# Forming a round's transposed rows by one set of products in the expert rounds of a two-block model kernel

## What is computed

```python
D_MODEL, MOE_EXPERTS, MOE_TOP_K, MOE_FF = 1024, 32, 2, 512
# every token goes to 2 of 32 experts; the tokens of an expert are its rows, padded to whole blocks
xp = jnp.zeros((nb * MOE_BLOCK, D), h.dtype).at[dest].set(h[tok_s])
def expert_block(args):
    xb, e = args
    return (jax.nn.silu(xb @ w_gate[e]) * (xb @ w_up[e])) @ w_down[e]
yp = lax.map(expert_block, ...)
return jax.ops.segment_sum(yp[dest] * w_s[:, None], tok_s, num_segments=T)
```

## Time and profile before

| | |
|---|---|
| median of 3 runs | 2140.02 us (2138.09 to 2142.48) |
| profiled execution | 2139.3 us, span on the core 2137.5 us |
| TensorE busy | 1995.6 us (93%), 9661 instructions |
| weight loads of TensorE | 1085.2 us (51%) |
| VectorE busy | 991.1 us (46%) |
| ScalarE busy | 683.1 us (32%) |
| GpSimd busy | 44.9 us (2%) |
| read from HBM | 605.06 MB, 289 GB/s over the span |
| chain that ended last | TensorE 68%, DMA 25%, VectorE 3%, ScalarE 2% |

### The profile page before, as it was taken

One profiled execution on the slowest core, in us unless ns is written; L12 is line 12 of the kernel. 1 busy time (PEld: TensorE's weight loads), 2 busy tenths in 40 slices (PEclk: granted clock), 3 DMA queues, 4 the chain that ended last, 5 costly groups with the idle time before them and its releaser, 6 DMA issues.

```text
span 2137.5 us, 29392 instructions
## 1 busy us (share of the span) xinstructions
PE 1995.6 (93%) x9661; PEld 1085.2 (51%) x9662; DVE 991.1 (46%) x2196; ACT 683.1 (32%) x1090; POOL 44.9 (2%) x80
## 2 busy tenths in 40 slices
PE   8999999999999999998999898888998999989888
PEld 4546777645577775554433343333774433334333
DVE  2375987303488544444444333344324443333335
ACT  1261000103400002142555444444202554444444
POOL 2000000000000000000000000001000000000000
PEclk9999999999999999999999999999999999999999
DMA  9505996533189543314999999999545999999996
GB/s 308 205 1 219 368 349 241 198 118 140 46 349 365 192 166 129 128 40 162 367 414 422 422 417 422 423 422 382 193 175 223 378 415 422 423 422 422 422 422 270
DMA packets 78511, 619.87 MB, mean 290 GB/s; under 512 B 9648, under 2 KB 9984, under 8 KB 15696
## 3 DMA queue, kind: packets, MB, share of 16 engines
q1 hardware_dynamic: 67824, 540.51, 63.0%
q0 software_dynamic: 6944, 66.33, 8.1%
q10 hardware_dynamic: 3648, 11.89, 1.4%
HBM read 605.06 MB, written 13.63 MB: 289 GB/s over the span
## 4 chain that ended last, share of the span: by engine, by line
PE 68%; DMA 25%; DVE 3%; ACT 2%; issue 1%; DVEq 0%; POOL 0%; SPq 0%; ACTq 0%; POOLq 0%
PE ps L851 26%; DMA big<-in_w_up 20%; PE ps L1093 14%; PE ps L1267 13%; PE ps L1105 7%; PE ps L865 3%; PE ps L1240 2%; PE ps L1269 2%; DMA big<-in_w_down 1%; DMA big<-in_w_gate 1%; ACT big L1774 1%; DMA big<-y_rows,big 1%; PE ps L1251 1%; DMA big<-in_dense 0%; DMA big<-in_first_final_g 0%
## 5 line engine op out<-in xcount | busy, mean ns | idle before, releaser
L1267 PE MATMUL ps<-big,hT 128*32 128x512 f32 x3072 | 698.3, 607 | 75.5 <-ACT big L1774 66.2
L1269 PE MATMUL ps<-big,hT 128*32 x1536 | 697.3, 607 | 0.0
L1774 ACT COPY big<-big 128x1024 f32 x384 | 396.8, 1046 | 483.2 <-PE ps L1269 294.4
L2513 DVE TENSOR_SCALAR big<-big 128x1024 f32 x384 | 265.3, 692 | 514.6 <-PE ps L1269 316.0
L1267 PEld LDWEIGHTS ps<-big,hT 128*32 128x32 f32 x3072 | 188.4, 111 | 450.1 <-issue 242.2
L1093 PE MATMUL ps<-hT,big 128*128 128x256 f32 x1408 | 311.2, 379 | 0.0
L851 PE MATMUL ps<-big,hT 128*128 128x512 f32 (+4 forms) x784 | 302.5, 537 | 4.0 <-ACT hT L1713 2.1
L1093 PEld LDWEIGHTS ps<-hT,big 128*128 128x128 f32 x1408 | 266.7, 190 | 49.4 <-issue 15.2
L851 PEld LDWEIGHTS ps<-big,hT 128*128 128x128 f32 x784 | 139.1, 192 | 132.4 <-issue 123.6
L1269 PEld LDWEIGHTS ps<-big,hT 128*32 128x32 f32 x1536 | 158.2, 111 | 6.2
L1105 PE MATMUL ps<-big 128*128 128x512 f32 x352 | 159.3, 595 | 0.7 <-DVE big L2277 0.7
(11 more groups left out here) (327 smaller groups left out, 1233.8 us busy)
## 6 DMA issues: line engine op xcount, KB each, us to landing
big<-in_w_gate SPq DMA_DIRECT2D x128, 1024.0 KB, 24.1
big<-in_w_up SPq DMA_DIRECT2D x128, 1024.0 KB, 23.2
big<-in_w_down SPq DMA_DIRECT2D x128, 1024.0 KB, 22.0
big<-in_dense SPq DMA_DIRECT2D x52, 1536.0 KB, 8.5
big<-in_dense POOLq DMA_DIRECT2D x28, 2048.0 KB, 10.0
big<-in_dense SPq DMA_DIRECT2D x21, 2048.0 KB, 7.9
y_rows<-c_res ACTq DMA_DIRECT2D x30, 384.0 KB, 7.0
big<-in_dense SPq DMA_DIRECT2D x5, 1024.0 KB, 36.6
```

What stands on the lines that cost most here:

```text
L1267: nc.tensor.matmul(ps[g * SLOTS:(g + 1) * SLOTS, bank, :], xT[:, k, g * SLOTS:(g + 1) * SLOTS], side[:, g - 1, quarter % 2, at:at + BW], s ...
L1269: return nc.tensor.matmul(ps[0:SLOTS, bank, :], xT[:, k, 0:SLOTS], experts3[:, bass.ds(here, 1), kind * CH + row:kind * CH + row + BW] .re ...
L1774: nc.scalar.copy(side[:, 1, quarter % 2, :], experts3[:, bass.ds(there, 1), lo:lo + QW] .rearrange("p a n -> p (a n)")).then_inc(s["side2_ ...
L2513: ts(side[:, 0, quarter % 2, :], experts3[:, bass.ds(there, 1), lo:lo + QW].rearrange("p a n -> p (a n)"), 1.0, None, mult).then_inc(s["si ...
```

## The change

A round's transposed rows are now formed directly. Where the rows of a round were `onehot` (stationary) times `fN` (moving), then copied and transposed, `rows_T` now takes for each of the 8 feature blocks k the columns k, k + 8, ... of `fN` as stationary operand (128 tokens by 128 features) and `onehot` (96 columns) as moving operand, over both token tiles. The result lands in the same PSUM places as the transposes did, and ScalarE copies it to `xeT` as before. `rows_of`, `row_half` on both engines, and the buffer `xe` are gone. The new products stand where `rows_of` stood, between the up product and the hidden transposes; nothing stands in the middle of the down product. ScalarE does its two copies to `xeT` after the tenth side copy of a round, ahead of the eleventh and twelfth, and in round 0 between its first and second side copy. Two waits of VectorE change their event (before `first_pick`) or go (`last_picks`). In routing, two small VectorE operations (`wsT`) move behind the block counts.

```diff
--- before.py
+++ after.py
@@ -265,7 +265,7 @@
             "out_done", "upper_landed_0", "upper_landed_1", "win_ready", "win_done", "cmp_zeroed", "hid_ready", "hid_copied", "fold_ready", "gelu_done",
             "kc_ready", "kc_done", "cmp_ready", "cmp_sub", "cmp_exp", "cmp_probs", "cmpT_ready", "cmpT_done",
             "up_ready", "up_copied", "conv_step", "conv_a", "conv_b", "silu_done", "gated", "aux_loaded",
-            "pick_step", "pick_ready", "rows_ready", "rows_copied_a", "rows_copied_v", "weights_picked", "last_turned", "xT_ready", "xT_done", "side1_copied", "side2_copied", "half_landed", "quarter_done",
+            "pick_step", "pick_ready", "weights_picked", "last_turned", "xT_ready", "xT_done", "side1_copied", "side2_copied", "half_landed", "quarter_done",
             "gate_silu", "hidden_done", "hT_ready", "hT_done", "y_ready", "y_stored",
             "route_pe", "route_dve", "route_act", "y_fetched_0", "y_fetched_1", "hot_ready", "last_ready",
             "last_spread", "combined", "gate_diags", "gate_ready", "gate_copied", "zeros_ready", "rows_zeroed", "diag_done",
@@ -384,7 +384,6 @@
         early_root = area(10240, 1)
 
         ym = c_res[:, 1, :]
-        xe = c_res[:, 0, :]
         onehot_w = c_res[:, 0, 0:2 * TC * ROWS].rearrange("p (k t r) -> p k t r", k=2, t=TC)
         hflat = hT[:].rearrange("p k n -> p (k n)")
         xeT = hflat[:, 0:KT * ROWS].rearrange("p (k n) -> p k n", k=KT)
@@ -592,8 +591,7 @@
                                     turned_a=2 * T, zdiag_done=1, z_ready=2, z_copied=2)
             st["route" + tag] = Stage(aux_loaded=64, route_pe=7, route_dve=7, route_act=1)
             st["moe" + tag] = Stage(
-                pick_step=T * nb, pick_ready=T * nb, rows_ready=2 * nb,
-                rows_copied_a=nb, rows_copied_v=nb, xT_ready=2 * nb, xT_done=2 * nb, side1_copied=12 * nb, side2_copied=12 * nb,
+                pick_step=T * nb, pick_ready=T * nb, xT_ready=2 * nb, xT_done=2 * nb, side1_copied=12 * nb, side2_copied=12 * nb,
                 half_landed=6 * nb, quarter_done=12 * nb,
                 gate_silu=nb, hidden_done=nb, hT_ready=2 * nb, hT_done=2 * nb, y_ready=nb - 1, y_stored=16 * (nb - 1))
             gate_stage("g2_" + tag, T // TC)
@@ -1230,27 +1228,18 @@
                 done, copied = s["quarter_done"], (s["side1_copied"], s["side2_copied"])
                 assert not owed[0]
 
-                def rows_of(b, first=False):
+                def rows_T(b, first=False):
 
                     pe.wait_ge(s["pick_ready"].sem, s["pick_ready"].at(b * TC + TC))
                     if not first:
                         pe.wait_ge(s["xT_done"].sem, s["xT_done"].at(b * 2))
-                    for h in range(2):
+                    for k in range(KT):
                         for t in range(T):
-                            ins = nc.tensor.matmul(ps[0:ROWS, h, :], onehot[:, t, :], fN[:, t, h * BW:(h + 1) * BW],
+                            rows = fN[:, t, :].rearrange("t (p k) -> t k p", k=KT)[:, k, :]
+                            ins = nc.tensor.matmul(ps[:, k // 4, k % 4 * ROWS:(k % 4 + 1) * ROWS], rows, onehot[:, t, :],
                                                    start=t == 0, stop=t == T - 1)
-                        ins.then_inc(s["rows_ready"].sem, 1)
-
-                def rows_T(b):
-
-                    pe.wait_ge(s["rows_copied_a"].sem, s["rows_copied_a"].at(b + 1))
-                    pe.wait_ge(s["rows_copied_v"].sem, s["rows_copied_v"].at(b + 1))
-                    for h in range(2):
-                        for k in range(4):
-                            rows = xe[0:ROWS, :].rearrange("t (p k) -> t k p", k=KT)[:, 4 * h + k, :]
-                            ins = nc.tensor.transpose(ps[:, h, k * ROWS:(k + 1) * ROWS], rows,
-                                                      const["ident"][0:ROWS, 0:ROWS])
-                        ins.then_inc(s["xT_ready"].sem, 1)
+                        if k % 4 == 3:
+                            ins.then_inc(s["xT_ready"].sem, 1)
 
                 def turn_last():
 
@@ -1287,7 +1276,7 @@
                                 ins = product(2 + kind, xeT, here, kind, quarter, k, FF, 0, k == 0, k == KT - 1)
                             ins.then_inc(done.sem, 1)
                     if more:
-                        rows_of(b + 1)
+                        rows_T(b + 1)
                     else:
                         turn_last()
                     for h in range(2):
@@ -1301,8 +1290,6 @@
                     if not first:
                         pe.wait_ge(s["y_ready"].sem, s["y_ready"].at(b))
                     for k in range(FFK):
-                        if k == 2 and more:
-                            rows_T(b + 1)
                         both_copied(b, 8 + k)
                         if k % 2 == 0:
                             pe.wait_ge(s["hT_done"].sem, s["hT_done"].at(b * 2 + (k // 2 + 1)))
@@ -1310,8 +1297,7 @@
                             ins = product(5 + h, hmT, here, 2, k, k, D, h * BW, k == 0, k == FFK - 1)
                         ins.then_inc(done.sem, 1)
 
-                rows_of(0, first=True)
-                rows_T(0)
+                rows_T(0, first=True)
                 after(pe, "ent" + name[-1], "route" + name[-1], "g2_" + name[-1])
                 turn(0, first=True)
                 with pe.Fori(1, ROUNDS - 1) as b:
@@ -1780,16 +1766,11 @@
                     act.wait_ge(s["y_ready"].sem, s["y_ready"].at(b + 1))
                     act.dma_start(rows[b * ROWS:(b + 1) * ROWS, :], ym[0:ROWS, :]).then_inc(s["y_stored"].sem, 16)
 
-                def row_half(b):
-                    act.wait_ge(s["rows_ready"].sem, s["rows_ready"].at(b * 2 + 1))
-                    nc.scalar.copy(xe[0:ROWS, 0:BW], ps[0:ROWS, 0, :]).then_inc(s["rows_copied_a"].sem, 1)
-
                 after(act, "route" + name[-1])
                 there = third(0)
                 copy(0, there, 0)
-                row_half(0)
+                rows_T(0)
                 copy(0, there, 1)
-                rows_T(0)
                 for b in range(ROUNDS):
                     for j in range(2, 4):
                         copy(b, there, j)
@@ -1802,12 +1783,11 @@
                         copy(b, there, j)
                     here = there
                     if b + 1 < ROUNDS:
-                        row_half(b + 1)
                         there = third(b + 1)
+                        rows_T(b + 1)
                     for j in range(10, 12):
                         copy(b, here, j)
                     if b + 1 < ROUNDS:
-                        rows_T(b + 1)
                         copy(b + 1, there, 0)
                         copy(b + 1, there, 1)
 
@@ -2422,13 +2402,13 @@
                 L(ins)
                 red(gwT, gw, add)
                 L(red(w2T.rearrange("p k t -> p (k t)"), by_k.rearrange("p k t e -> p (k t) e"), add))
-                L(tt(wsT, w2T[:, 0], w2T[:, 1], add))
-                L(tt(wsT, wsT, sum_[:, 0:TC], mult))
 
                 v.wait_ge(s["route_pe"].sem, s["route_pe"].at(4))
                 L(ts(nb_i[0:E, :], ps[0:E, 2, 0:P], float(SLOTS - 1), None, add))
                 L(ts(nb_i[0:E, :], nb_i[0:E, :], SLOTS.bit_length() - 1, None, ALU.logical_shift_right))
                 ts(nbT[0:E, :], nb_i[0:E, :], 1.0, None, ALU.max).then_inc(step, 1)
+                L(tt(wsT, w2T[:, 0], w2T[:, 1], add))
+                L(tt(wsT, wsT, sum_[:, 0:TC], mult))
                 L(nc.vector.reciprocal(wrT, wsT))
                 L(tt(wrT, wrT, gwT, mult))
                 for k in range(2):
@@ -2461,11 +2441,6 @@
                 nc.vector.tensor_copy(tab_i, ps[0:1, 5, 0:256].rearrange("p (a b) -> p a b", a=4)[:, :, 0:NB])\
                     .then_inc(step, 1)
 
-            def row_half(s, b):
-
-                v.wait_ge(s["rows_ready"].sem, s["rows_ready"].at(b * 2 + 2))
-                nc.vector.tensor_copy(xe[0:ROWS, BW:D], ps[0:ROWS, 1, :]).then_inc(s["rows_copied_v"].sem, 1)
-
             def first_pick(s, b):
 
                 for t in range(TC):
@@ -2531,12 +2506,10 @@
                     first, last, following = b == 0, b == ROUNDS - 1, (None, None)
                     for j in range(9):
                         copy(b, there, loads, j, first)
-                        if j == 1 and first:
-                            row_half(s, 0)
                         if j == 1 and not first:
                             rows_out(b - 1)
                         if j == 3 and not last:
-                            v.wait_ge(s["rows_ready"].sem, s["rows_ready"].at(b * 2 + 2))
+                            v.wait_ge(s["xT_ready"].sem, s["xT_ready"].at(b * 2 + 2))
                             first_pick(s, b + 1)
                         if j == 4 and not last:
                             second_pick(s, b + 1)
@@ -2554,7 +2527,6 @@
                                               ps[:, 4 + 3 * h, 0:2 * ROWS].rearrange("p (a b) -> p a b", a=2))\
```

(2 more changed lines are left out.)

## The result

The changed kernel takes 2187.18 us (median of 4 runs, 2186.15 to 2189.15) against 2141.25 us for the kernel before (4 runs), a ratio of 1.0214 with a 95% interval of 1.0199 to 1.0229. It is 46 us slower where 9 us less were forecast. The profiled execution has a span of 2185.5 us, 48 us more than before.

A forecast was written before the change was run, and what follows sets the result against it. The prediction took weight transfer to bound both expert stages, with TensorE counting where it makes the transfer pause. Savings of 4.8 + 3.8 + 0.3 = 8.9 us gave 2130.4 us for the profiled execution, 2131.0 as median, range 2127 to 2138.

The forecast's parts named there:

- What bounds the kernel: Both expert stages: each is one long weight transfer at 422 GB/s; TensorE counts where it makes that transfer pause.
- the later pauses that were named: Transfer pauses after each stage's first: worth 1.5, 1.0 and 0.7 us in the first stage, 1.4 and 1.1 in the second.
- The new products: On TensorE each round: 32 instructions 0.1115 us apart, 3.57 us, the weight load setting the pace with or without stride.
- The high end of 0.192 us: Upper bound for one new product on TensorE: load plus product without overlap, 0.111 + 0.081 us, 6.1 us a round.
- the saving of 1.0 us a round: Per TensorE-bound round: 4.57 us of row products and transposes removed, 3.57 us of new products added.
- The start: First stage, from first row product to first expert product: 4.53 us instead of 6.39, 1.86 us saved.
- The 0.25 us of the reordering: In routing, moving two small VectorE operations behind the block count frees 0.25 us, between ends of 0 and 0.26.
- (C): All 32 new products of each round: strided loads take 0.204 us each, 6.5 us a round; 2153.5 us, chance 0.09.
- (A): Only the stage starts come earlier, by 2.1 and 1.8 us; later pauses stay as wide; 2136.1 us, chance 0.13.
- (B): In the stages the transfer hides all of the gain, weights already queued at the start deciding; 2140 us, chance 0.04.
- (D): Down stretch behind round 14 counts in full, first-round pauses shrink too: 1.0 + 1.0 us more, 2128.5 us, chance 0.12.
- The sum: First stage 4.8 us, second stage 3.8, end of the first stage 0.3: 8.9 us saved, 2131.0 us as median.

The follow-up runs named there:

- The kernel in block order: The changed kernel with token features written in block order by their last writers, so each stationary block is 128 neighbouring elements: 2134.42 us, 0.9971 of the kernel before.
- the experiment with plain products: The kernel before with its eight strided transposes written as ordinary products with the identity, 16 instructions instead of 8: 2188.22 us (one run).

## Why the prediction was wrong, point by point

**What bounds the kernel** was read rightly: a stage is a weight transfer, and TensorE counts where it lets it pause. The kernel in block order nearly closed just the later pauses that were named.

**The new products** are the step that failed. The pace of 0.1115 us was taken from two neighbours, each with one of the two properties of the new loads: ordinary, but contiguous (the router), and strided, but transposed. They were taken to bound the case that is ordinary and strided at once; they don't, as the experiment with plain products shows. The high end of 0.192 us was a sum of load and product and below the 0.238 measured too. The argument that loads and products overlap was right (0.111 us with contiguous blocks) and beside the point: loads 0.238 us apart do not hide behind products of 0.08 us. The term stood at 3.57 us a round and measured 7.87; the saving of 1.0 us a round became a loss of 7.87 - 4.57 = 3.3 us.

**The start** was forecast to be 1.86 us shorter and is 8.51 against 6.39 us. It fails by the same term; with blocks in order and the clock up it is 4.38 us.

**The 0.25 us of the reordering** is too small for these times, but VectorE's own rows show it. From the start of the last reduction ahead of the block counts to the operation behind the wait it takes 2.36 us before (from 1007.29 us) and 2.14 in block order (from 1007.29 us too): 0.22 us. In the profile of the changed kernel it is 2.35, as the block counts wait 0.25 us for TensorE there.

**The rivals.** (C) is what happened: place, side and, in the main, mechanism. The stride slows the loads of ordinary blocks, but not to their recorded length, as (C) had it: that is 335 ns, and they follow each other by 238. Its size was off twice. Its price of 0.204 us was the length of a load of the transposes, where 0.238 was measured, 1.1 us a round more. And it let the loss act at the start and in two rounds of each stage, and at one later pause of the first. With rounds of 30.7 us TensorE bounds nearly the whole stage, so the loss acts in nearly all rounds; from the first row product to the last expert product stage 1 became 31.2 us longer, stage 2 19.5 us. A third part, the clock, was in no rival: 1.2 to 1.3 us a round, by the estimate above some two thirds of the 27.6 us between 2187 and 2160. (A) and (B) are out by the kernel in block order: the later pauses nearly closed and the time fell. (D) has nothing for it, and its time does not add up either: 2.0 us under 2131.0 is 2129.0, not 2128.5. (C) had been given 0.09 because rows of another kind of instruction, the transposes, did not show the loss.

**The sum** of the forecast holds otherwise in the main. With the one term as assumed (0.111 us) the runs give 2134.4 us, where 2131.0 was said with a range of 2127 to 2138; rounds of 25.4 where 25.3 was said. Of the 9 us forecast this is 6.

## What to carry to other kernels

Let a stationary fp32 block of an ordinary product lie in neighbouring elements, or at most every second one; where the last writer of the data can put them in that order off the chain, this is cheap (2187 to 2134 us here, although the writers took up to 0.7 us longer an operation). A row bounds a new instruction only if it has all of its properties at once; that a transpose tolerates a layout says nothing of a product. And a burst of such slow loads (0.233 us apart and more) was paid twice here, for itself and in the clock of what follows.

## What the runs showed of the hardware

Loads of a 128-column fp32 block for ordinary products follow each other by 0.111, 0.118, 0.174, 0.233 and 0.238 us with steps of 1, 2, 3, 4 and 8 elements; for transposes with a step of 8 by 0.109 us. The slow pace does not depend on the clock: the 32 products of the changed kernel keep 0.24 us across its fall from 0.97 to 0.50, while contiguous ones go from 0.111 to about 0.21 us at the lower level (the 5.44 us above against 3.81). The granted clock fell in or behind the slow products of nearly every round, with TensorE listed as busy in 5.00 of 5.00 us before it; with twice as many contiguous products it stayed at 1.00, and with loads 0.174 us apart at 0.99.
